# Two-tile and one-tile experts interleaved, some weight pieces left unsplit, and modulation chunks redistributed, in a two-block transformer kernel

## The reference

```python
for i in range(DEPTH):                      # first block, DEPTH = 2
    shift, scale, gate = ada_modulation(c, ada_w[i, 0], ada_b[i, 0])
    h = x * (1.0 + scale) + shift
    y = windowed_gqa(...) if i % 2 == 0 else recurrent_block(...)
    x = layer_norm(DN_ALPHA * x + (1.0 + gate) * y, ln_g[i, 0], ln_b[i, 0])
    shift, scale, gate = ada_modulation(c, ada_w[i, 1], ada_b[i, 1])
    y = sq_relu_mlp(x * (1.0 + scale) + shift, mlp_w1[i], mlp_w2[i])
    x = layer_norm(DN_ALPHA * x + (1.0 + gate) * y, ln_g[i, 1], ln_b[i, 1])
...
def moe_ffn(h, router_w, router_b, w_gate, w_up, w_down):
    ...                                     # top 2 experts inside the best of 4 groups
    for e in range(N_EXPERTS):
        he = (jax.nn.silu(h @ w_gate[e]) * (h @ w_up[e])) @ w_down[e]
        out = out + combine[:, e:e + 1] * he.astype(jnp.float32)
```

## Time and profile before

| | |
|---|---|
| median of 3 runs | 1654.36 us (1653.45 to 1654.6) |
| the profiled execution | 1654.29 us, span of its trace 1653.0 us |
| PE busy | 1363.9 us (83%), mean granted clock 0.925 |
| DVE busy | 1159.7 us (70%) |
| ACT busy | 719.7 us (44%) |
| DMA | 311.91 MB, mean 189 GB/s |
| attention, from scores to the end of its layer norm | about 90 to 212 us |
| first MLP, recurrent layer, second MLP | about 212 to 404, to 627, to 870 us |
| second block up to the experts | to about 1234 us |
| experts and final norm | to 1653 us |

### The profile page before, as it was taken

One profiled execution on the slowest core, in us unless ns is written; L12 is line 12 of the kernel. 1 busy time (PEld: TensorE's weight loads), 2 busy tenths in 40 slices (PEclk: granted clock), 3 DMA queues, 4 the chain that ended last, 5 costly groups with the idle time before them and its releaser, 6 DMA issues.

```text
span 1653.0 us, 20870 instructions
## 1 busy us (share of the span) xinstructions
PE 1363.9 (83%) x7808; PEld 1182.8 (72%) x7808; DVE 1159.7 (70%) x1541; ACT 719.7 (44%) x896; POOL 63.4 (4%) x54
## 2 busy tenths in 40 slices
PE   0862889998999987998974998665789999999995
PEld 0752789997777766998963787654677887776774
DVE  6657677777586656887886647886565556888885
ACT  2332344443467673444432433210234445776763
POOL 2100010000100001000000000330000000000000
PEclk9975989999999988999986999987879999999998
DMA  9425577775566536766660345100044555888891
GB/s 355 153 77 196 173 236 279 258 264 206 178 214 211 200 102 235 269 223 229 223 242 8 118 161 194 62 1 10 1 150 139 182 186 189 304 313 309 307 316 75
DMA packets 84070, 311.91 MB, mean 189 GB/s; under 512 B 9344, under 2 KB 9568, under 8 KB 83360
## 3 DMA queue, kind: packets, MB, share of 16 engines
q1 hardware_dynamic: 82080, 298.88, 51.4%
q10 hardware_dynamic: 1888, 11.69, 2.1%
HBM read 309.48 MB, written 1.05 MB: 188 GB/s over the span
## 4 chain that ended last, share of the span: by engine, by line
PE 61%; DVE 29%; ACT 6%; issue 2%; DMA 1%; DVEq 0%; POOL 0%; ACTq 0%; SPq 0%; POOLq 0%
PE ps L390 60%; DVE w_low L349 8%; DVE junk L349 6%; ACT w_high L349 2%; DVE t_one L349 1%; DVE t_two L349 1%; DVE x L349 1%; DMA ring<-stream 1%; DVE rs L349 1%; DVE he L349 1%; DVE r_two L349 1%; DVE qp L349 1%; DVE pf L349 1%; ACT h_high L349 1%; DVE sc L349 1%
## 5 line engine op out<-in xcount | busy, mean ns | idle before, releaser
L349 DVE TENSOR_TENSOR w_low<-ring,w_high 128x1024 fp32r<-128x1024 f32 x376 | 461.7, 1228 | 167.1 <-ACT w_high L349 138.1
L349 ACT ACTIVATE w_high<-ring 128x1024 fp32r<-128x1024 f32 x376 | 398.8, 1061 | 303.6 <-PE ps L390 173.9
L390 PE MATMUL ps<-x_high,w_high 128*128 128x256 f32 (+1 forms) x784 | 236.6, 302 | 82.6 <-DVE x_low L349 71.7
L390 PE MATMUL ps<-x_low,w_high 128*128 128x256 f32 (+1 forms) x784 | 233.5, 298 | 0.0
L390 PE MATMUL ps<-x_high,w_low 128*128 128x256 f32 (+1 forms) x784 | 233.3, 298 | 0.0
L390 PEld LDWEIGHTS ps<-x_high,w_high 128*128 128x128 f32 x784 | 155.0, 198 | 94.5 <-issue 88.3
L349 DVE CUSTOM_DVE_ANT_0 junk<-ring,cond 128x1024 f32<-128x1024 f32 x133 | 165.9, 1247 | 20.5 <-DMA ring<-stream 2.6
L390 PEld LDWEIGHTS ps<-x_low,w_high 128*128 128x128 f32 x784 | 155.1, 198 | 2.5
L390 PEld LDWEIGHTS ps<-x_high,w_low 128*128 128x128 f32 x784 | 154.8, 197 | 2.8
L390 PE MATMUL ps<-h_high,w_high 128*128 128x256 f32 x512 | 145.9, 285 | 3.7 <-DVE w_low L349 2.3
L390 PE MATMUL ps<-h_low,w_high 128*128 128x256 f32 x512 | 145.0, 283 | 0.0
(11 more groups left out here) (299 smaller groups left out, 2156.6 us busy)
## 6 DMA issues: line engine op xcount, KB each, us to landing
ring<-stream SPq DMA_DIRECT2D x376, 512.0 KB, 4.8
ring<-moe SPq DMA_DIRECT2D x192, 512.0 KB, 4.7
tab_two<-tab ACTq DMA_DIRECT2D x1, 2824.0 KB, 14.3
gw<-gw ACTq DMA_DIRECT2D x1, 2304.0 KB, 13.4
cond<-cvec ACTq DMA_DIRECT2D x3, 512.0 KB, 6.6
x<-xT ACTq DMA_DIRECT2D x1, 1024.0 KB, 11.7
ctx<-ctxT ACTq DMA_DIRECT2D x1, 1024.0 KB, 4.8
pos<-posT ACTq DMA_DIRECT2D x1, 1024.0 KB, 6.9
```

The costliest lines, as they stand in the source:

```text
L349: return op(*a, **k).then_inc(self.sem, 1)
L390: return pe.matmul(out, stationary, moving, start=start, stop=stop, skip_group_check=True)
```

## The change

Five things are changed.

1. Attention's `w_out` is used unsplit. OT is not split either: o_high and o_low are gone, and PE does 64 plain float32 matmuls.
2. Attention does 8 modulation chunks instead of 12 between its batches, and the other 4 during its output projection; `low_upto(W_MLP0 + 4)` on DVE now stands behind the whole projection.
3. The recurrent layer does 16 chunks instead of 12 (the four added are single-condition chunks of the second block), and the second MLP 12 instead of 16, by the table A2_TURNS: its turns have 1, 2, 1, 2, 2, 2, 2 and 0 chunks.
4. The 16 expert places are taken in the order EXPERTS, (group, expert): one two-tile expert, then three one-tile experts. The results of two-tile experts are no longer accumulated in PSUM over four experts but summed in SBUF by DVE (`sums`); those of one-tile groups stay in PSUM banks 4 and 5 until their fourth expert.
5. ACT computes SiLU directly, and DVE's multiply `gates` is gone. The last of the four down pieces of a one-tile expert is used unsplit (`e_whole`). Before a one-tile expert PE does two gate pieces instead of one ahead of `turn`.

```diff
-A2_ORDER = [0, 8, 1, 9, 2, 10, 3, 11, 4, 12, 5, 13, 6, 7] + list(range(14, 24))
+A2_TURNS = ((0,), (1, 12), (2,), (3, 13), (4, 14), (5, 15), (6, 7), ())
+A2_ORDER = [8, 9, 10, 11] + [c for turn in A2_TURNS for c in turn] + list(range(16, 24))
...
+EXPERTS = ((0, 0), (1, 0), (1, 1), (1, 2), (0, 1), (1, 3), (2, 0), (2, 1), (0, 2), (2, 2), (2, 3), (3, 0), (0, 3), (3, 1), (3, 2), (3, 3))
+
+SCATTERS = {7: 1, 12: 2, 14: 0}
+SCATTER_ORDER = (1, 2, 0, 3)
...
-    order = pieces("a" * 8 + "w" * 6 + "a" * 12 + "w" * 4 + mlp)
+    order = pieces("a" * 8 + "w" * 6 + "a" * 8 + "wa" * 4 + mlp)
     for b in range(NB):
-        order += "aa" * (b < 12) + "ww" * (b < 14) + "w" * (b >= 3)
+        order += "aa" + "ww" * (b < 14) + "w" * (b >= 3)
+    mlp = "ww" + "".join("w" + "a" * (len(turn) > 0) + "w" + "a" * (len(turn) > 1) + "ww" for turn in A2_TURNS)
...
-SPLIT = [w for w in range(W_END) if not W_RNN <= w < W_MLP1]
+WHOLE = [W_ATT <= w < W_MLP0 or W_RNN <= w < W_MLP1 for w in range(W_END)]
+for _p in range(16):
+    WHOLE[MOE_AT[_p, "d", 3]] = EXPERTS[_p][0] > 0
+SPLIT = [w for w in range(W_END) if not WHOLE[w]]
...
@@ load_program
-            if kind == "w" and W_RNN <= n < W_MLP1:
+            if kind == "w" and WHOLE[n]:
                 sp.wait_ge(s.used, n + 1)
...
@@ tensor_program
-    pe.wait_ge(s.o_low, 2)
-    project(W_ATT, m.OTS)
+    pe.wait_ge(s.ot, 4)
+    for n in range(KT):
+        piece = whole(W_ATT + n)
+        for k in range(KT):
+            ins = mm(PS[:, 4 + n // 2, (n % 2) * 256:(n % 2 + 1) * 256], piece[:, k * P:(k + 1) * P], m.OT[:, k, :], k == 0, k == KT - 1)
+        ins.then_inc(s.used, 1)
...
@@ tensor_program, down
+            if i > 0 and n == 3:
+                piece = whole(w)
+                pe.wait_ge(s.e_whole, singles_upto(p))
+                for half in range(2):
+                    ins = mm(PS[:, 4 + half, :], m.HW, piece[:, half * 512:(half + 1) * 512], False, j == 3)
+                ins.then_inc(s.used, 1)
+                continue
...
     for p in range(NE):
         if p < NE - 1:
-            gate(p + 1, 0, 1)
+            head = 1 if EXPERTS[p + 1][0] == 0 else 2
+            gate(p + 1, 0, head)
         turn(p)
         if p < NE - 1:
-            gate(p + 1, 1, 4)
+            gate(p + 1, head, 4)
...
@@ scalar_program
-            A(m.SGe[:, a, :], PS[:, a, :], ACT.Sigmoid, s.sig)
+            if p > 0:
+                act.wait_ge(s.h, tiles_upto(p - 1))
+            A(m.SGe[:, a, :], PS[:, a, :], ACT.Silu, s.silu)
...
@@ vector_program, attention
-        for _ in range(3):
+        for _ in range(2):
             modulation(m.junk)
...
-    project(W_ATT, m.gate1)
+    for n2 in range(4):
+        modulation(m.junk)
+        vv.wait_ge(s.used, W_ATT + 2 * n2 + 2)
+        for n in (2 * n2, 2 * n2 + 1):
+            add_branch(n, PS[:, 4 + n2, (n % 2) * 256:(n % 2 + 1) * 256], m.gate1[:, n:n + 1])
+    bias(24, 16, "ada_b", 24)
+    low_upto(W_MLP0 + 4)
...
@@ vector_program, experts
-    def gates(p):
-        for a in range(len(tiles_of(p))):
-            vv.wait_ge(s.sig, tiles_upto(p - 1) + a + 1)
-            op(vv.tensor_tensor, m.SGe[:, a, :], m.SGe[:, a, :], PS[:, a, :], ALU.mult, inc=s.silu)
...
+    def sums(p):
+
+        if EXPERTS[p][0] == 0 and EXPERTS[p][1] > 0:
+            vv.wait_ge(s.used, MOE_AT[p, "d", 3] + 1)
+            vv.wait_ge(s.y_out, 2)
+            op(vv.tensor_tensor, m.YE[:, 0, :], m.YE[:, 0, :], PS[:, 6:8, :].rearrange("p c n -> p (c n)"), ALU.add, inc=s.y_add)
+            for c in range(2):
+                half = m.YE[:, 1, c * 512:(c + 1) * 512]
+                op(vv.tensor_tensor, half, half, PS[:, 1 + 2 * c, :], ALU.add, inc=s.y_add if c else None)
```

More of the change, by code:

```diff
@@ L153 @@
     t2 x_high x_low x_add x_next
-    qk_out rope_mm rope_ps qk v_out score_mm sc smax exp prob pt_mm pt pv_mm o_high o_low
+    qk_out rope_mm rope_ps qk v_out score_mm sc smax exp prob pt_mm pt pv_mm ot
     mean_mm xc sq var_mm root
@@ L218, in __init__ @@
         self.OT = kt(view("ot", a0 + 7168, 2048))
-        self.OTS = (kt(rounded("o_high", a0 + 9216, 2048)), kt(rounded("o_low", a0 + 11264, 2048)))
         self.RT = view("rt", a0 + 13312, 512, 32)
@@ L410, in out_tile, with whole @@
         ins.then_inc(s.used, 1)
+    def whole(w):
+        c = W_AT[w]
+        pe.wait_ge(arrived[c % RING], 16 * (c // RING + 1))
+        return m.piece(c)
     def second_product(w, src_half, first, p=P):
@@ L534, in tensor_program @@
     layer_norm(1)
-    def whole(w):
-        c = W_AT[w]
-        pe.wait_ge(arrived[c % RING], 16 * (c // RING + 1))
-        return m.piece(c)
     def z_of(b):
@@ L836, in hidden @@
                     pe.wait_ge(s.xg_low, n + 1)
+                if p == 1 and kind == "g":
+                    pe.wait_ge(s.xg_low, 4 + k + 1)
                 slots = slice(tile * P, (tile + 1) * P)
@@ L1492, in mlp @@
             t, w = t0 + i, w0 + 8 * i
+            chunks = len(A2_TURNS[t - 8]) if t >= 8 else 2
             low_upto(w + 5)
@@ L1517, in vector_program @@
     layer_norm(1, 2, 56, 48, ALPHA)
+    vv.wait_ge(s.silu_c2, 1)
     op(vv.memset, m.XP[:, :, 0:2], 0.0)
@@ L1561, in vector_program @@
             z_of(b + 2)
+    modulation(m.junk_rnn, conditions())
     scan_pair(NB // 2 - 1)
@@ L1912, in vector_program @@
     for p in range(NE):
-        w = MOE_AT.get((p + 1, "g", 0), W_END)
+        w = MOE_AT[p, "d", 0] - 4
+        back = SCATTERS.get(p + 1)
         if p > 0:
-            low_upto(w + (4 if p < 4 else 1))
+            low_upto(w + 3)
             products(p)
-        low_upto(w + (5 if p < 4 else 3))
-        turned(p)
-        if p < NE - 1:
-            for r in range(4):
-                low_upto(w + 3 + r)
-                if p >= 4 and p % 4 == 0:
-                    results(p // 4 - 1, r)
-            if p < 4:
-                low_upto(w + 8)
-            gates(p + 1)
-            if p < 4:
-                low_upto(w + 12)
+        low_upto(w + 4)
+        if back is not None:
+            results(back, 0)
+        low_upto(w + 5)
+        if back is not None:
+            results(back, 1)
+        turned(p)
+        low_upto(w + 6)
+        if back is not None:
+            results(back, 2)
+        low_upto(w + 7)
+        if back is not None:
+            results(back, 3)
+        low_upto(w + 12)
+        sums(p)
     for r in range(4):
```

142 lines of the change are left out of this document (86 added, 56 removed).

## The result

The changed kernel takes 1610.34 us in the median (1609.61 to 1610.53), beside 1654.48 for the kernel before on the same chip: ratio 0.973, 95% interval 0.9715 to 0.974. That is 44.1 us less; 35.4 were forecast, and the range of 1603 to 1637 held it. The profiled execution's span is 1608.9, 44.1 under the 1653.0 of before, so the two traces can be compared stage by stage. Each mark is the start of one instruction that both kernels have; DVE's first step of a layer norm is rs.

The account below looks back on a forecast made before the run. No single engine was taken as the bound (chain 61% PE, 29% DVE, 6% ACT). Attention -15.5, recurrent layer +1.9, second MLP -7.2 and experts -14.6 sum to -35.4: 1654.3 to 1618.9 us, range 1603 to 1637.

Parts of the forecast that it names:

- The loads did not become the bound: Experts, first rival: loads bound one-tile experts, 19.1 us each instead of 17.5, 18.8 more in all, 1637 us; chance 0.20.
- Rival 2: Attention: projection at half clock throughout, 57 us instead of 31.9, total 1644 us; chance 0.07.
- rival 3: Experts: SP's wait at a whole piece empties the pipeline, 22.3 us per one-tile expert against 17.5, total 1676; chance 0.04.
- The fit that the forecast took: Experts' loads: fixed 2.0 us plus size over 436 GB/s, a piece landing in 3.2 us; sum would be 1616.5.
- A, attention: Attention to its layer norm: -24.1 from earlier projection, +5.7 for unsplit products, +2.9 for weight splits behind; -15.5 us.
- After a similar idle stretch I expect the same again: Attention's projection: the same 3.2 us half-clock loss at its start, so 26.2 becomes 31.9, +5.7 us.
- B, recurrent layer: Added modulation chunks: all halves hidden by DVE but the last two, before the last scan steps; +1.9 us.
- C, second MLP: Fewer modulation chunks: turns 0 and 2 and the last turn's two chunks, 1.8 per chunk; -7.2 us.
- D, experts: Experts: -13.4 us from first to last he, and -1.2 from PE's wait for the last he; -14.6 in all.
- the stalls: Experts: PE stalls expected to stay, 12.8 us beside 341.5 of PE work, giving 354.3 from first to last he.
- The stall of he behind the adds of sums: Experts: next splits late behind three adds over 2048 columns, 0.7 + 2.0 x 3 us within the stalls.
- the loads' part: Experts: refilling a whole piece's slot takes 7.0 against PE's 6.8, losing 0.2 us per one-tile expert, 2.4 in all.

Follow-up runs that it names:

- e_hold: Changed kernel with the fourth down piece of one-tile experts split again, but SP waiting for PE there as if it were unsplit; 1610.21 us.
- att12: Changed kernel with attention's 12 modulation chunks between the batches as before and w_out still unsplit; 1616.07 us.
- rnn15: Changed kernel with the recurrent layer's last modulation chunk moved to the second MLP's last turn; 1605.94 us.
- rnn_fill: Changed kernel with eight unused identity products on PE in its wait before the recurrent layer's second last output group; 1609.09 us.
- e_both: Changed kernel with the fourth down piece of one-tile experts split again and the gate multiply back on DVE; 1610.06 us.
- ln_fill38: Changed kernel with 38 unused identity products on PE behind the sums of the layer norms before both MLPs; 1610.11 us.

## Why the prediction was right, and where it was not

**The sign, and most of the size.** 35.4 of 44.1 were forecast. That the measured time lies in the range is in part luck: attention and the experts gave 13.8 more than forecast, and three other stages took 5.2 more. Several of the signs that I had named did not come: the clock of the projection's first 10 us was 1.00 and not 0.7, rs came at 174.00 and not after 175, h_low of the second MLP's turns 0 and 2 stood 23.6 apart and not 23.0, and first to last he was 347.8 and not 354. None of the rivals came. The loads did not become the bound: neighbours are 18.1 apart on average, not 19.1, at 331 GB/s. Rival 2 had the clock the wrong way round, and rival 3, SP's hold, exists but costs about 3.5 us in all instead of 57.6. The Trainium skill, "DMA: Bandwidth & Descriptors", in its section on the anatomy of one DMA, puts a wait on the issuing sequencer before dispatch. The trace agrees: SP stood 44.3 us for PE and ACT's waits for loads rose from 12.1 to 28.0. e_hold then shows the loss without any unsplit piece. The fit that the forecast took from the same section is given there for DMAs that GpSimd issues; the pieces here are issued by SP and landed in 4.6 us in the median, not 3.2.

**A, attention: -22.6 instead of -15.5.** The step that failed is "After a similar idle stretch I expect the same again". The idle stretch was not similar: 0.69 before the projection (the forecast's own arithmetic had removed the 13.17) and 0.61 before the last batch. The projection took 27.9 instead of 31.9, -4.0. The same clock took 2.6 from the last transposes and V products, which I had priced as unchanged, and with the scores 0.9 earlier the projection began at 139.42 instead of 143.1. att12 tells it apart: with 3.14 of standing still the V products take 3.79 again. In all eleven profiles with this attention PE waits 0.38 to 0.61 there, and V products and projection take 2.05 and 27.89. The wait behind the projection, 6.7 from its end to rs, was priced at 6.2.

**B, recurrent layer: +4.5 instead of +1.9.** The term of the sum was right for DVE and for PE's wait (2.0 measured) and left out what the wait does: 32 records at half clock, +3.3, together 5.2 at that place, of which 0.7 comes back elsewhere in the stage. Shown twice, by removing the wait (rnn15) and by filling it (rnn_fill). As it happens I priced the clock where PE's wait went away as if it had stayed, and not at all where a wait was added; the two errors have opposite sign and partly cancel.

**C, second MLP: -7.0 instead of -7.2.** A chunk less gives 1.27 a turn and not 1.8, and why not is open. It isn't the amount of DVE's work: DVE is busy 17.5 in turn 0 (635.33 to 658.90), as in a turn of the first MLP that takes 23.04. The last turn's two chunks give 3.2 up to evacuate and 1.2 more by the clock (PE's sums behind evacuate, 3.14 then 1.92 of DVE's waiting). The total is right and its parts are not.

**Second block: +1.9 instead of 0.** Nothing is changed there. 1.6 of it is one group of transposes that took half clock after and full clock before, at the same place of the program and behind the same wait. Before, then after:

```profile
1018.34 1.97 PE L661 MATMUL ps<-ident,kc 128*128 128x128 f32 x16 [3.60 <-DVE kc L349]
```

```profile
991.88 3.68 PE L682 MATMUL ps<-ident,kc 128*128 128x128 f32 x16 [3.60 <-DVE kc L365]
```

So the length of a wait alone doesn't decide whether the clock is lost; what does is open, and I didn't test it. In the experiments, where this block is unchanged too, it takes 383.1 to 383.5 in four profiles, 384.8 to 385.4 in seven and 381.8 in one (e_both).

**D, experts: -20.1 instead of -13.4.** The term that was mis-sized is the stalls: 12.8 in the forecast, 347.8 - 341.5 = 6.3 measured. The stall of he behind the adds of sums, 2.0 each, hardly came: a one-tile and a two-tile expert together take 52.9, 1.4 above their work of 51.5, where my stalls of 0.7 and 2.0 made 54.2. (The working of the loads' part was loose as well: five pieces at 1.36, not six, give its 6.8, and of its 2.4 only 8 x 0.2 = 1.6 stand in the stalls.) The largest single piece is the last place. Before, DVE at the last he, then after:

```profile
1614.99 6.54 DVE L349 TENSOR_TENSOR w_low<-ring,w_high 128x1024 fp32r<-128x1024 f32 x5
1621.63 0.75 DVE L349 SCALAR_TENSOR_TENSOR he<-sge,rout,ps 128x512 f32<-128x512 f32 x1
```

```profile
1574.33 1.23 DVE L365 TENSOR_TENSOR w_low<-ring,w_high 128x1024 fp32r<-128x1024 f32 x1 [0.26 <-ACT w_high L365]
1578.93 0.75 DVE L365 SCALAR_TENSOR_TENSOR he<-sge,rout,ps 128x512 f32<-128x512 f32 x1 [3.38 <-PE ps L406]
```

The last he stood behind five splits; now DVE splits only up to the third piece of up ahead of it (low_upto(w + 3)), and DVE waits for PE. The last interval shrank by 6.6, from 22.39 to 15.82. About half of it is this: PE's wait between its last up product and the last turn fell from 4.32 to 0.84. The other half is that in the new kernel he of the place before stands behind splits, some 2.6 us after its own last product, so that the marks show more than PE gained. I had seen PE's wait of 4.32 and put -1.2 on the unsplit piece for it, where it was the place of he in DVE's list: in e_both, where the piece is split, PE waits 0.84 as well.

And the mechanism that I named for the gain, DVE's relief by SiLU and the unsplit piece, is not what gave it. e_both has neither and keeps 18.7 of 20.1. Why the order gives what it does is only partly shown: quiet neighbours went from 18.90 to 18.43 with the same DVE work, the last place explains some 3.5, and a one-tile expert beside a two-tile one takes 52.7 with it, of which 51.0 is work. The parts (sums in SBUF, two gate pieces ahead of turn, DVE's and ACT's new orders) were not taken back alone. With the old order of the experts they could not all stay, since two two-tile experts in a row would need the same PSUM banks.

## What to carry to other kernels

When a change makes PE's wait shorter or longer, price the clock of the work behind it, in both directions: here a wait of 2.6 us instead of 0.6 cost 3.3 us more than itself, and a projection that no longer followed a wait ran 4 us faster than forecast. Give that price a chance and not a certainty: behind a wait of 3.60 us the same transposes ran once at full and once at half clock. An operation left unsplit, or any buffer released later, also holds the queue that refills it: look at what is loaded next before counting the relief. Two edits that relieve the same engine don't add once it is no longer the bound, so take them out one at a time.

## What was not expected of the hardware

PE's clock fell to half after waits as short as 2.5 to 3.1 us (2.54, 2.57, 2.67 and 3.14 above), and it stayed up after single waits of 0.4 to 0.9. Neither holds everywhere: one wait of 3.60 us cost it nothing in the kernel before, and at the end of the changed kernel's experts two waits close together, 0.84 and 1.43, went ahead of products at a mean of 0.73. It also ran at half in V products 1.1 us behind transposes that ran at full (138.05 and 140.26 in att12), so the fall can come after the wait, inside the work that follows. Products of the identity with no use kept it up as well as others do (rnn_fill, ln_fill38). The Trainium skill, "TensorE: Matmul & The Clock Gate", in its section on oscillation, describes a kernel that falls back to half clock at each wait for data; the rows here agree for most waits on DVE of 2.5 us and more, and not for that of 3.60 us.
